# A gdn inverse on 64 by 64 diagonal blocks in quadrants of TensorE's array, and a narrower use of GpSimd for weight low parts

## The chip, the cores and the metric

The kernel is one launch on one core of a Trainium2 chip. The metric is the device time of the launch in microseconds, the median of several runs. Engines are named PE (TensorE, matmuls), PEld (its weight loads), DVE (VectorE), ACT (ScalarE), POOL (GpSimd) and SP (which issues most of the DMAs). SBUF is the on-chip memory of 128 partitions, PSUM the memory that TensorE writes, 8 banks of 128 partitions by 512 floats.

## The reference, cut to what matters

Two models run one after the other on one sequence of 256 tokens with 1024 channels. The first has four layers: gdn (gated delta rule), hgrn, gla, gdn. The second has two layers, here called "four", because four mixers share one projection. Each layer is a projection, a mixer, an output projection, a norm and a gated feed-forward part.

```
def chunk_gated_delta_rule(q, k, v, beta, g):            # the gdn mixer, 8 heads
    ...
    G = jnp.cumsum(g, axis=-1)
    decay = jnp.exp(jnp.where(incl, G[..., :, None] - G[..., None, :], -jnp.inf))
    kb = k * beta[..., None]
    L = jnp.where(strict, jnp.einsum('bhncd,bhnsd->bhncs', kb, k) * decay, 0.0)
    rhs = jnp.concatenate([v * beta[..., None], kb * jnp.exp(G)[..., None]], axis=-1)
    sol = lax.linalg.triangular_solve(L + jnp.eye(CHUNK), rhs, left_side=True, lower=True)
    ...
```

The kernel works with chunks of 128 tokens instead of 64, so it inverts, for each of 8 heads and 2 chunks, the unit lower triangular matrix I + L of 128 by 128: 16 matrices, called problems below.

## The kernel before, in words

**Order of work.** Each engine has its own program, written out by hand, and waits on semaphores that the other engines count up. There is no planner: an engine runs its instructions strictly in the order of the text. `CHAIN` lists the layers: gdn, hgrn, gla, gdn, four, four.

**Projections.** The weights come in units of up to 128 by 2048 floats into a ring of six buffers. Every product is made from three: high part times high part, low times high and high times low, with a weight split into `w_hi` (rounded) and `w_lo` (what is left). The cast to the high part is made by ACT or DVE (`hi_by`, in `unit_plan`), into one of three slots, so it waits until TensorE is done with the unit three before. The low part, ring minus high, is split between two engines: `low_share` eighths of its columns are made by DVE (`split` in the vector program, L1933) and the rest by POOL (`split` in the gpsimd program, L1373). The plan before: from the fourth unit of a layer's projection on (`n >= HI`), DVE casts and makes 2 eighths of the low part, POOL 6 eighths, in every kind of layer. The first three units are cast by ACT, and so are the units of the feed-forward part; there DVE makes the whole low part. TensorE's three products of a unit are at L513 (`products`) and L541 (`token_products`). In hgrn and gla DVE's splits are placed by hand between the steps of its decay work (`due`); in gdn and four they stand ahead of the convolution of the unit that TensorE has finished. ACT's `cast` stands ahead of its work on a unit's output, and does nothing where DVE casts.

**The inverse in a gdn layer.** For each head DVE makes `lt` (the transposed L, 128 by 384 for both chunks and the block across them), from TensorE's products and ACT's Exp. Then the inverse X is built by doubling: at level lv the diagonal blocks of size 2^lv are already inverted, and those of 2^(lv+1) follow. The 16 problems go in four groups g of four. A level has, per group:

- POOL: `masked`, lt times a mask of the level, 128 by 512, into `ct` (L1406); it waits for the cx of the level before;
- PE: `cx` (L881), masked lt times the first halves of X's columns, 64 columns of output per problem;
- ACT: copies cx to `yb`, 128 by 256 (L1413);
- PE: the correction `z` (`gdn_correct`, L952), X transposed times that;
- DVE: subtracts it from X, 128 by 256 (L1887);
- PE: transposes X (`gdn_transpose`, L940), 128 by 128 per problem;
- ACT: copies that to the transposed X in `inv`, 128 by 512 (L1413).

Level 0 has only the mask, DVE's identity minus mask (`first_inverse`) and the transposes. Level 6 has no transposes; it works with the blocks of 64 by 64 (L884, L954), and its correction goes straight into the transposed X. On PE the groups are interleaved: cx of group 0, cx 1, z 0, cx 2, z 1, transposed 0, cx 3, z 2, transposed 1, z 3, transposed 2, transposed 3. `stay_awake` issues matmuls that nothing uses, in places where PE would stand (L585).

Of the kernel before, what the change touches and what calls it, by code (L numbers as in the profile page):

```python
# [29 lines left out]
P = 128  # L30
T = 256
# [181 lines left out]
def build(nc, A, out, book, layers=len(CHAIN)):  # L213

    book.restart()
    with ExitStack() as ctx:
# [42 lines left out]
        ones_d = sb("ones_d", [P, P])  # L259
# [4 lines left out]
        level = sb("level", [P, 7, P])  # L264

# [68 lines left out]
        cx = flat(yb)[:, 0:16 * HALF2].rearrange("p (j n) -> p j n", j=16)  # L334

# [3 lines left out]

        def first_halves(ap, lv):  # L340

            dims = " ".join("abc"[:len(ap.shape) - 2])
            r = ap.rearrange(f"p {dims} (n two c) -> p {dims} n two c", two=2, c=1 << lv)
            return r[:, :, 0, :] if len(ap.shape) == 2 else r[:, :, :, 0, :]
# [141 lines left out]
        def _(pe):  # L486
# [353 lines left out]
            def gdn(layer):  # L840
# [32 lines left out]
                for lv in range(1, 7):  # L873
                    for g in range(4):
                        b = psum.claim(pe, "cx", layer, lv, g)
                        pe.wait_ge(*pool_gdn.at("masked", layer, lv, g))
                        pe.wait_ge(*(act_gdn.at("X", layer, g) if lv == 1 else dve_gdn.at("X", layer, lv - 1, g)))
                        for j in range(4 * g, 4 * g + 4):
                            cols_of = slice((j % 4) * HALF2, (j % 4 + 1) * HALF2)
                            if lv < 6:  # L880
                                m = nc.tensor.matmul(b[:, cols_of].rearrange("p (n c) -> p n c", c=1 << lv),  # L881
                                                     ct[:, j, :], first_halves(inv[:, j, :], lv), start=True, stop=True)
                            else:
                                m = nc.tensor.matmul(b[HALF2:HALF, cols_of], ct[0:HALF2, j, HALF2:HALF], inv[0:HALF2, j, 0:HALF2],  # L884
# [50 lines left out]
            def gdn_transpose(layer, lv, g):  # L935
# [373 lines left out]
        def _(pool):  # L1309
# [21 lines left out]
            fill(ones_d[:, :], 1.0 / D)  # L1331
# [62 lines left out]
            for layer, (kind, _) in enumerate(CHAIN[:layers]):  # L1394
# [6 lines left out]
                for lv in range(7):  # L1401
                    for q in (0, 2, 1, 3) if lv == 0 else range(4):
                        t, h0 = q // 2, 4 * (q % 2)
                        pool.wait_ge(*(dve_gdn.at("lt", layer, h0 + 3) if lv == 0 else
                                       dve_gdn.at("XT", layer, 0, q) if lv == 1 else pe_gdn.at("cx", layer, lv - 1, q)))
                        g.tensor_tensor(ct[:, 4 * q:4 * q + 4, :], lt[:, h0:h0 + 4, t * T:t * T + HALF],  # L1406
                                        level[:, lv:lv + 1, :].to_broadcast([P, 4, HALF]), ALU.mult)\
# [1173 lines left out]
```

## Time and profile before

| | us |
|---|---|
| median of 3 runs (lowest, highest) | 2332.07 (2331.16, 2338.66) |
| the profiled execution | 2331.76 |
| its span, first to last instruction | 2330.1 |
| PE busy | 2213.6 (95%) |
| DVE busy | 1527.5 (66%) |
| ACT busy | 873.9 (38%) |
| POOL busy | 407.5 (17%) |
| mean granted TensorE clock | 0.972 |

The profile is one execution. Busy time is per engine, and engines overlap, so the shares don't add up to the span. A fp32 matmul stands as two records (two passes), and records of matmuls overlap in their durations, so the distance between starts tells what one costs. The granted clock is a share of full speed: 1.00 is 2.4 GHz, 0.50 is 1.2 GHz. The chain of waits goes back from the last instruction to what released it, and so on.

### The profile page before, as it was taken

How to read it: one execution, taken by the hardware profiler on the slowest of the kernel's cores; microseconds unless marked ns; L12 is line 12 of the kernel's file. 1: busy time of each engine (PE TensorE's matmuls, PEld its weight loads, DVE VectorE, ACT ScalarE, POOL GpSimd, SP SyncE). 2: the span in 40 equal slices, each digit the busy share in tenths (PEclk: the TensorE clock that was granted, in tenths of full speed). 3: DMA queues.
4: the chain of work that ended last, by engine and by line, in shares of the span. 5: the costliest groups of instructions: out<-in, count | busy, mean ns of one | idle time of the engine just before them, and what ended most of it. 6: DMA issues, size and time to landing. Idle time of an engine off the chain costs nothing.

```text
span 2330.1 us, 33338 instructions
## 1 busy us (share of the span) xinstructions
PE 2213.6 (95%) x13185; PEld 1915.0 (82%) x13185; DVE 1527.5 (66%) x1923; ACT 873.9 (38%) x1160; POOL 407.5 (17%) x227
## 2 busy tenths in 40 slices
PE   7999999999999999999899999989889999978999
PEld 7988788898788788788798978869568997847998
DVE  7854744797754668645785285466567887367886
ACT  3344444331344322444314444432554333354332
POOL 6632000160000050000262300005120002330000
PEclk9999999999999999999999999999889999979999
DMA  7510565552565443655451056545115554403552
GB/s 213 176 37 25 193 190 189 167 186 64 167 193 182 160 161 97 199 187 174 145 181 55 1 173 194 183 145 165 51 51 173 190 182 134 154 6 114 190 188 91
DMA packets 265597, 333.67 MB, mean 143 GB/s; under 512 B 16492, under 2 KB 228593, under 8 KB 265473
## 3 DMA queue, kind: packets, MB, share of 16 engines
q1 hardware_dynamic: 265473, 331.93, 44.5%
q8 instruction: 89, 1.46, 0.3%
q14 instruction: 35, 0.29, 0.0%
HBM read 330.84 MB, written 1.05 MB: 142 GB/s over the span
## 4 chain that ended last, share of the span: by engine, by line
PE 85%; DVE 9%; ACT 3%; issue 2%; POOL 1%; DVEq 0%; POOLq 0%; ACTq 0%
PE bank L541 42%; PE bank L513 27%; PE bank L952 2%; PE bank L881 2%; PE bank L585 1%; PE bank L1009 1%; DVE w_hi L1931 1%; PE bank L575 1%; PE bank L732 1%; PE bank L940 1%; ACT w_hi L1459 1%; ACT mats L1413 1%; ACT xh L1413 1%; DVE w_lo L1933 1%; PE bank L838 1%
## 5 line engine op out<-in xcount | busy, mean ns | idle before, releaser
L1933 DVE TENSOR_TENSOR w_lo<-ring,w_hi 128x2048 fp32r<-128x2048 f32 (+3 forms) x297 | 561.9, 1893 | 328.5 <-ACT w_hi L1459 325.3
L1459 ACT ACTIVATE w_hi<-ring 128x2048 fp32r<-128x2048 f32 x204 | 385.5, 1890 | 463.2 <-PE bank L541 298.8
L1373 POOL TENSOR_TENSOR w_lo<-ring,w_hi 128x1536 fp32r<-128x1536 f32 (+3 forms) x71 | 277.1, 3903 | 1436.2 <-DVE w_hi L1931 1436.2
L541 PE MATMUL bank<-w_lo,xh 128*128 128x512 f32 x992 | 268.9, 393 | 1.5 <-POOL w_lo L1373 1.4
L541 PE MATMUL bank<-w_hi,xh 128*128 128x512 f32 x928 | 250.9, 392 | 10.6 <-ACT xh L1413 6.8
L513 PE MATMUL bank<-xh,w_lo 128*128 128x256 f32 (+2 forms) x1880 | 246.2, 284 | 5.0 <-POOL w_lo L1373 5.0
L541 PE MATMUL bank<-w_hi,xl 128*128 128x512 f32 x928 | 249.0, 390 | 0.0
L513 PE MATMUL bank<-xh,w_hi 128*128 128x256 f32 (+1 forms) x1816 | 242.7, 287 | 2.3 <-DVE w_hi L1931 2.3
L513 PEld LDWEIGHTS bank<-xh,w_lo 128*128 128x128 f32 (+2 forms) x1880 | 232.2, 188 | 8.0 <-issue 5.7
L513 PEld LDWEIGHTS bank<-xh,w_hi 128*128 128x128 f32 (+1 forms) x1816 | 229.9, 192 | 9.2 <-issue 5.5
L513 PE MATMUL bank<-xl,w_hi 128*128 128x256 f32 (+1 forms) x1816 | 237.2, 283 | 0.0
L513 PEld LDWEIGHTS bank<-xl,w_hi 128*128 128x128 f32 (+1 forms) x1816 | 225.7, 190 | 0.7
L541 PEld LDWEIGHTS bank<-w_lo,xh 128*128 128x128 f32 x992 | 185.8, 189 | 40.6 <-issue 3.0
L541 PEld LDWEIGHTS bank<-w_hi,xh 128*128 128x128 f32 x928 | 173.2, 188 | 50.0 <-issue 11.6
L541 PEld LDWEIGHTS bank<-w_hi,xl 128*128 128x128 f32 x928 | 174.7, 188 | 36.7
L1931 DVE CAST w_hi<-ring 128x2048 fp32r<-128x2048 f32 (+2 forms) x93 | 160.2, 1723 | 43.9 <-PE bank L513 22.9
L541 PE MATMUL bank<-w_hi,hid_hi 128*128 128x512 f32 x528 | 169.0, 401 | 8.1 <-DVE hid_lo L1887 8.1
L541 PE MATMUL bank<-w_hi,hid_lo 128*128 128x512 f32 x528 | 165.0, 394 | 0.0
L541 PE MATMUL bank<-w_lo,hid_hi 128*128 128x512 f32 x528 | 164.4, 393 | 0.0
L1413 ACT ACTIVATE yb<-bank 128x256 f32<-128x256 f32 (+4 forms) x146 | 59.0, 404 | 162.1 <-PE bank L541 124.9
L541 PEld LDWEIGHTS bank<-w_lo,hid_hi 128*128 128x128 f32 x528 | 100.3, 190 | 21.9
L541 PEld LDWEIGHTS bank<-w_hi,hid_lo 128*128 128x128 f32 x528 | 100.0, 189 | 21.9
(310 smaller groups left out, 2605.6 us busy)
## 6 DMA issues: line engine op xcount, KB each, us to landing
ring<-in_ffn_w_in_dram SPq DMA_DIRECT2D x264, 512.0 KB, 4.5
ring<-in_ffn_w_down_dram SPq DMA_DIRECT2D x88, 512.0 KB, 4.3
ring<-in_gdn_w_in_dram SPq DMA_DIRECT2D x64, 512.0 KB, 5.2
ring<-in_ffn_w_out_dram SPq DMA_DIRECT2D x44, 512.0 KB, 4.2
ring<-in_w_in_dram SPq DMA_DIRECT2D x36, 512.0 KB, 4.6
ring<-in_hgrn_w_in_dram SPq DMA_DIRECT2D x32, 512.0 KB, 4.8
ring<-in_gla_w_in_dram SPq DMA_DIRECT2D x24, 512.0 KB, 4.2
ring<-in_gdn_w_out_dram SPq DMA_DIRECT2D x16, 512.0 KB, 4.0
```

Source lines behind the costliest of these rows:

```text
L513: m = nc.tensor.matmul(cols, *((wk, xk) if tokens == ALL else (xk, wk)), start=(first and step == 0 and k == 0 and (j % 2 == 0)), stop=(la ...
L541: m = nc.tensor.matmul(bank[:, 0:width], xin[:, k0 + k, rows_of], w[:, k, c * width:(c + 1) * width], start=(first and step == 0 and k == ...
L575: m = nc.tensor.transpose(b[:, j * P:(j + 1) * P], src[:, t, c * CHUNK + j * P:c * CHUNK + (j + 1) * P], ident[:, :])
L585: m = nc.tensor.matmul(b[:, 0:T], ones[:, :], strict[:, 0:T], start=True, stop=True)
L732: m = nc.tensor.transpose(banks[6][:, j * T + t * HALF:j * T + (t + 1) * HALF], hidt[:, t, j * P:(j + 1) * P], ident[:, :])
L881: m = nc.tensor.matmul(b[:, cols_of].rearrange("p (n c) -> p n c", c=1 << lv), ct[:, j, :], first_halves(inv[:, j, :], lv), start=True, st ...
L952: m = nc.tensor.matmul(b[:, cols], inv[:, 16 + j, :], cx[:, j, :], start=True, stop=True)
L1373: g.tensor_tensor(w_lo[:, unit % RING, part], ring[:, unit % RING, part], high_part(unit)[:, part], ALU.subtract).then_inc(*pool_lo.tick())
L1413: nc.scalar.activation(out_, in_, func, **kw).then_inc(*sig.tick(*key))
L1459: nc.scalar.activation(high_part(u)[:, 0:n], ring[:, u % RING, 0:n], ACT.Copy).then_inc(*act_hi.tick())
L1931: v.tensor_copy(high[:, 0:n], w[:, 0:n]).then_inc(*dve_hi.tick())
L1933: v.tensor_tensor(w_lo[:, u % RING, 0:share], w[:, 0:share], high[:, 0:share], ALU.subtract).then_inc(*dve_lo.tick())
```

## The change

The plan for units: POOL makes low parts only in gdn layers; elsewhere DVE makes all of a unit's low part. In four layers ACT makes all casts. The inverse: up to level 5 only the two 64 by 64 blocks on the diagonal of each problem are kept and worked on, block 0 in partitions 0 to 63 and block 1 in partitions 64 to 127, packed as 64 columns per problem (`xb`, `xtb`, `lb`, `lb_masked`). A matmul of 128 by 128 becomes two of 64 by 64, one in each diagonal quadrant of the array, both into the same PSUM bank. POOL's masks, ACT's copies and DVE's first subtraction are of half the size (128 by 256). ACT copies the diagonal blocks out of lt (8 copies per layer); POOL clears the transposed X; after level 5 ACT spreads the transposed blocks into 128 by 128 tiles, two copies per group. The second block is transposed by a matmul with the identity. Level 6 reads lt itself and doesn't wait for a mask.

```diff
-                unit_plan(KT * w, "dve" if n >= HI else "act", 2 if n >= HI else 8 if layer else 4)
+                unit_plan(KT * w, "act" if n < HI or kind == "four" else "dve", 2 if n >= HI and kind == "gdn" else 8 if layer else 4)
...
+        blocks = (slice(0, HALF2), slice(HALF2, HALF))
+        xb, xtb = (flat(inv[:, 8 * n:8 * n + 8, :]).rearrange("p (j n) -> p j n", j=16) for n in range(2))
+        lb_masked, lb = (flat(ct)[:, 16 * HALF2 * n:16 * HALF2 * (n + 1)].rearrange("p (j n) -> p j n", j=16) for n in range(2))
...
-                        pe.wait_ge(*pool_gdn.at("masked", layer, lv, g))
+                        if lv < 6:
+                            pe.wait_ge(*pool_gdn.at("masked", layer, lv, g))
...
-                                m = nc.tensor.matmul(b[:, cols_of].rearrange("p (n c) -> p n c", c=1 << lv),
-                                                     ct[:, j, :], first_halves(inv[:, j, :], lv), start=True, stop=True)
+                                for r in blocks:
+                                    m = nc.tensor.matmul(b[r, cols_of], lb_masked[r, j, :], xb[r, j, :], start=True, stop=True)
...
-                    m = nc.tensor.transpose(b[:, (j % 4) * P:(j % 4 + 1) * P], inv[:, j + (16 if lv == 0 else 0), :], ident[:, :])
+                    cols_of, src = slice((j % 4) * HALF2, (j % 4 + 1) * HALF2), xtb if lv == 0 else xb
+                    nc.tensor.transpose(b[blocks[0], cols_of], src[blocks[0], j, :], ident[blocks[0], blocks[0]])
+                    m = nc.tensor.matmul(b[blocks[1], cols_of], src[blocks[1], j, :], ident[blocks[1], blocks[1]], start=True, stop=True)
...
-                        m = nc.tensor.matmul(b[:, cols], inv[:, 16 + j, :], cx[:, j, :], start=True, stop=True)
+                        for r in blocks:
+                            m = nc.tensor.matmul(b[r, cols], xtb[r, j, :], cx[r, j, :], start=True, stop=True)
...
-            fill(ones_d[:, :], 1.0 / D)
...
-                for lv in range(7):
+                pool.wait_ge(*act_gdn.at("decay", layer, 0))
+                g.memset(inv[:, 16:32, 0:HALF2], 0.0).then_inc(*pool_gdn.tick("cleared", layer))
+                for lv in range(6):
...
-                        g.tensor_tensor(ct[:, 4 * q:4 * q + 4, :], lt[:, h0:h0 + 4, t * T:t * T + HALF],
-                                        level[:, lv:lv + 1, :].to_broadcast([P, 4, HALF]), ALU.mult)\
+                        g.tensor_tensor(lb_masked[:, 4 * q:4 * q + 4, :], lb[:, 4 * q:4 * q + 4, :],
+                                        level64[:, lv:lv + 1, :].to_broadcast([P, 4, HALF2]), ALU.mult)\
...
+                def diagonal_blocks(g):
+                    t0, h0 = (g // 2) * T, 4 * (g % 2)
+                    act.wait_ge(*dve_gdn.at("lt", layer, h0 + 3))
+                    for r in blocks:
+                        run(s, lb[r, 4 * g:4 * g + 4, :], lt[r, h0:h0 + 4, t0 + r.start:t0 + r.stop], ACT.Copy, "blocks", layer, g)
+
                 for h in range(8):
...
+                    if h in (5, 7):
+                        for g in ((0, 2) if h == 5 else (1, 3)):
+                            diagonal_blocks(g)
...
+                    if lv < 5:
+                        dst, key = (xb, ("X", layer)) if lv == 0 else (xtb, ("XT", layer, lv))
+                        run(s, flat(dst[:, 4 * g:4 * g + 4, :]), b, ACT.Copy, *key, g)
+                    else:
+                        for r in blocks:
+                            run(s, inv[r, 16 + 4 * g:16 + 4 * g + 4, r], b[r, :].rearrange("p (h n) -> p h n", h=4), ACT.Copy, "XT", layer, lv, g)
...
-                            XT = inv[0:HALF2, 16 + 4 * g:16 + 4 * g + 4, HALF2:HALF]
-                            tt(s, XT, XT, b[0:HALF2], ALU.subtract, "XT", layer, lv, g)
+                            ts(s, inv[0:HALF2, 16 + 4 * g:16 + 4 * g + 4, HALF2:HALF], b[0:HALF2].rearrange("p (h n) -> p h n", h=4), -1.0, ALU.mult,
+                               None, None, "XT", layer, lv, g)
```

VectorE's setup also gets four small copies, which pack the identity and the masks to 64 columns.

## Rows read from the trace of the kernel before

**Rows 1.** The page, busy time by engine: us (share of span) xinstructions.
```profile
PE 2213.6 (95%) x13185; PEld 1915.0 (82%) x13185; DVE 1527.5 (66%) x1923; ACT 873.9 (38%) x1160; POOL 407.5 (17%) x227
```

**Rows 2.** Busy time by stretches: from:to, length, engines, PEclk, DMA share, GB/s.
```profile
156.00:165.10 9.10, 8.94 (x83) 8.73 (x81) 1.69 (x4) 3.93 (x8) 7.79 (x7) 1.00 0.00 0
...
1265.00:1271.00 6.00, 4.12 (x25) 3.13 (x25) 4.68 (x5) 1.68 (x3) 5.13 (x4) 1.00 0.01 3
1271.00:1288.00 17.00, 17.00 (x84) 16.88 (x83) 1.69 (x4) 3.75 (x8) 8.17 (x7) 0.50 0.00 0
```

**Rows 3.** Groups by shape, 151.8 to 205.4 us: xcount, busy, mean ns, idle before.
```profile
L952 PE MATMUL bank<-yb,inv 128*128 128x64 f32 x160 | 20.9, 273 | 0.0
...
L940 PE MATMUL bank<-ident,inv 128*128 128x128 f32 x96 | 14.6, 276 | 2.7 <-DVE inv L1887 2.6
...
L1413 ACT ACTIVATE yb<-bank 128x256 f32<-128x256 f32 x20 | 7.7, 384 | 12.0 <-PE bank L881 12.0
```

**Rows 4.** Chain of waits through the levels: start us, us, what.
```profile
156.06 1.74 PE bank L881 x16
...
163.09 0.85 PE bank L952 x8
...
163.97 0.43 DVE inv L1887
...
164.54 0.63 PE bank L940 x4
...
201.58 1.07 PE bank L884 x16
...
1271.65 3.31 PE bank L881 x16
...
1324.70 1.07 PE bank L884 x16
```

**Rows 5.** Stretches of level 6, PE and PEld, L884 alone (two), then L954.
```profile
201.50:202.60 1.10, 1.09 (x16) 1.00 (x16) 1.00 0.00 0
203.00:203.90 0.90, 0.90 (x14) 0.86 (x15) 1.00 0.00 0
...
203.00:203.90 0.90, 0.90 (x15) 0.76 (x12) 1.00 0.00 0
```

**Rows 6.** Chain of waits at the entry of the first inverse.
```profile
150.57 1.28 POOL ct L1406
...
151.87 3.43 DVE inv L1887 x2
```

**Rows 7.** Timeline, ScalarE among the scores: start, us, instruction [idle before].
```profile
145.44 0.52 ACT L1413 ACTIVATE dec<-dec 128x384 f32<-128x384 f32 x1 [1.63 <-DVE dec L1897]
```

**Rows 8.** Timeline of hgrn's projection: DVE, then PE, then POOL.
```profile
448.77 2.28 DVE L1933 TENSOR_TENSOR w_lo<-ring,w_hi 128x2048 fp32r<-128x2048 f32 x1
450.97 1.22 DVE L1931 CAST w_hi<-ring 128x2048 fp32r<-128x2048 f32 x1
...
452.83 4.54 DVE L1931 CAST w_hi<-ring 128x2048 fp32r<-128x2048 f32 x1
...
529.29 2.96 PE L513 MATMUL bank<-xh,w_hi 128*128 128x256 f32 x16 [2.29 <-DVE w_hi L1931]
...
457.45 4.02 POOL L1373 TENSOR_TENSOR w_lo<-ring,w_hi 128x1536 fp32r<-128x1536 f32 x1 [1.16 <-DVE w_hi L1931]
```

**Rows 9.** Timeline of gla's projection: PE, then DVE.
```profile
847.06 2.05 PE L541 MATMUL bank<-w_lo,xh 128*128 128x512 f32 x4 [1.39 <-POOL w_lo L1373]
...
842.91 0.69 DVE L1933 TENSOR_TENSOR w_lo<-ring,w_hi 128x512 fp32r<-128x512 f32 x1
```

**Rows 10.** Chain of waits: a four layer's projection, and a cast on ScalarE.
```profile
1551.10 1.91 ACT w_hi L1459
...
1585.74 54.44 PE bank L513 x456
```

More of the change, by code:

```diff
@@ L334, in build, with bank64 @@
         cx = flat(yb)[:, 0:16 * HALF2].rearrange("p (j n) -> p j n", j=16)
+        blocks = (slice(0, HALF2), slice(HALF2, HALF))
+        xb, xtb = (flat(inv[:, 8 * n:8 * n + 8, :]).rearrange("p (j n) -> p j n", j=16) for n in range(2))
+        lb_masked, lb = (flat(ct)[:, 16 * HALF2 * n:16 * HALF2 * (n + 1)].rearrange("p (j n) -> p j n", j=16) for n in range(2))
+        def bank64(bank):
+            return bank[:, 0:4 * HALF2]
         def prob(n):
             return lt[:, 4 + n % 4, :]
[L340 to L344, printed above, removed]
         def block_ratio(lv, heads):
@@ L1693, in gdn @@
                     run(s, d, d, ACT.Exp, "decay", layer, h)
+                    if h in (5, 7):
+                        for g in ((0, 2) if h == 5 else (1, 3)):
+                            diagonal_blocks(g)
                 def transposed(lv, g):
                     act.wait_ge(*pe_gdn.at("transposed", layer, lv, g))
-                    dst, key = (four_tiles(inv, g), ("X",)) if lv == 0 else (four_tiles(inv, 4 + g), ("XT",))
-                    run(s, dst, psum.bank("transposed", layer, lv, g)[:, :], ACT.Copy, *key, layer, *([lv] if lv else []), g)
+                    b = bank64(psum.bank("transposed", layer, lv, g))
+                    if lv < 5:
[4 more added lines that the diff above has]
+                            run(s, inv[r, 16 + 4 * g:16 + 4 * g + 4, r], b[r, :].rearrange("p (h n) -> p h n", h=4), ACT.Copy, "XT", layer, lv, g)
                     psum.release(s, "transposed", layer, lv, g)
@@ L1949, in setup @@
                 v.tensor_copy(pick[:, :], ident[0:8, 0:8]).then_inc(*s.tick("pick"))
+                for r in blocks:
+                    v.tensor_copy(ident64[r, :], ident[r, r]).then_inc(*s.tick())
+                    v.tensor_copy(level64[r, :, :], level[r, 0:6, r]).then_inc(*s.tick())
                 v.tensor_copy(trig[:, 0, :], pos_i).then_inc(*s.tick())
@@ L2222, in first_inverse @@
                     dve.wait_ge(*pool_gdn.at("masked", layer, 0, g))
-                    tt(s, inv[:, 16 + 4 * g:16 + 4 * g + 4, :], ident[:, :].rearrange("p (a n) -> p a n", a=1).to_broadcast([P, 4, P]),
-                       ct[:, 4 * g:4 * g + 4, :], ALU.subtract, "XT", layer, 0, g)
+                    tt(s, xtb[:, 4 * g:4 * g + 4, :], ident64[:, :].rearrange("p (a n) -> p a n", a=1).to_broadcast([P, 4, HALF2]),
+                       lb_masked[:, 4 * g:4 * g + 4, :], ALU.subtract, "XT", layer, 0, g)
                 for h in range(8):
@@ L2244, in gdn @@
                         dve.wait_ge(*pe_gdn.at("z", layer, lv, g))
-                        b = psum.bank("z", layer, lv, g)[:, 0:4 * HALF2].rearrange("p (h n) -> p h n", h=4)
+                        b = bank64(psum.bank("z", layer, lv, g))
                         if lv < 6:
-                            X = first_halves(inv[:, 4 * g:4 * g + 4, :], lv)
-                            tt(s, X, X, b.rearrange("p h (n c) -> p h n c", c=1 << lv), ALU.subtract, "X", layer, lv, g)
-                        else:
-                            XT = inv[0:HALF2, 16 + 4 * g:16 + 4 * g + 4, HALF2:HALF]
-                            tt(s, XT, XT, b[0:HALF2], ALU.subtract, "XT", layer, lv, g)
+                            X = flat(xb[:, 4 * g:4 * g + 4, :])
+                            tt(s, X, X, b, ALU.subtract, "X", layer, lv, g)
+                        else:
+                            ts(s, inv[0:HALF2, 16 + 4 * g:16 + 4 * g + 4, HALF2:HALF], b[0:HALF2].rearrange("p (h n) -> p h n", h=4), -1.0, ALU.mult,
+                               None, None, "XT", layer, lv, g)
                         psum.release(s, "z", layer, lv, g)
```

9 lines of the change are left out of this document (5 added, 4 removed).

## The prediction

> **What bounds the kernel now.** I read the page first: TensorE is busy 95% of the span [rows 1]. So time is to be had only where TensorE works at something that can be made smaller, or where it stands. The edited code touches two kinds of stretch: the triangular inverse of the two gdn layers, and the projections of the hgrn, gla and four layers. Next the table by stretches [rows 2]: in a level of the first layer's inverse TensorE is busy 8.94 of 9.10 us, so TensorE bounds it. In the second gdn layer the same work runs 17 us at a granted clock of 0.50 (the 1.2 GHz level), right after an entry in which TensorE was busy 4.12 of 6 us. Third the groups of that stretch by shape [rows 3]: what a level is made of. Fourth the chain of waits through the levels [rows 4]: levels 1 to 5 run from 156.06 to 201.58 in the first gdn layer, 45.5 us, and from 1271.65 to 1324.70 in the second, 53.05 us.
>
> **The change part by part.**
>
> *A level of the inverse, before.* An fp32 matmul is two records, a transpose one. The correction has 160 records in 5 levels, cx as many, the transposes 96 in 6 [rows 3]: a level has 32 + 32 + 16 = 80. In the chain 16 records of cx take 1.74 [rows 4], 0.11 us each. 80 x 0.11 = 8.8, plus some 0.3 of waiting: the 9.1 seen.
>
> *A level after.* Each product becomes two of 64 x 64, one in rows and columns 0 to 63, one in 64 to 127: 64 records for cx, 64 for the correction, and 16 transposes + 16 matmuls with the identity = 48, in all 176. What one costs hangs on whether the two quadrants work at the same time. The sixth level already works in quadrants (the two others, crosswise) [rows 5]: alone, 16 records take 1.09 us, 0.068 each; where the two products meet, 14 and 15 records of them lie in the same 0.90 us, 0.062 a pair. I take 0.06 a pair. A group of cx or of the correction then is 8 pairs, 0.48 us (before 0.87); a transposed group is bound by its lower quadrant, 8 records, 0.48 (before 4 x 0.11). Twelve groups give 5.8 us of TensorE a level.
>
> Now the waits, which a shorter TensorE uncovers. From [rows 4]: the level's last correction begins at 163.09, has its 8 records issued 0.11 x 8 later, and VectorE takes it up at 163.97: not over 0.2 us after issue is over, I take 0.2. VectorE runs 0.43, and TensorE starts at 164.54: 0.77 us in all. ScalarE's copy of 128 x 256 takes 0.38 [rows 3], so 0.72. Walking the issue order (cx0, cx1, z0, cx2, z1, T0, cx3, z2, T1, z3, T2, T3): z0 waits for cx0's copy, ready at 0.48 + 0.72 = 1.20 instead of 0.96: 0.24 lost. The other corrections have a group or more between. T3 follows z3 by one group, 0.48, and needs 0.77: 0.29 lost. Level: 5.8 + 0.5 = 6.3 us. ScalarE has 8 copies, 3.0 us, VectorE 4 x 0.43, GpSimd 4 masks at half of 1.28 [rows 6]: all below 6.3, and a mask needs only a cx of the level before. Five levels are 31.5 us: 14.0 saved in the first gdn layer, 21.5 in the second if its clock stays at 1.00. Bounds of a level: 5.5 (nothing waits) and 11.8 (no pair overlaps: 176 x 0.067).
>
> The overlap seen in [rows 5] is of two quadrants that write two banks; here both write one, and no row shows that. The Trainium skill (TensorEngine Tiling, Restrictions and Gotchas) says that different row tiles cannot access the same bank at the same time. By that rule the level would be the upper bound. Its page on PSUM (PSUM bank collisions) lets accesses to different 32-partition quadrants of one bank run side by side, which is this case; by that it is 6.3.
>
> *Entry of the inverse.* Before: behind the last lt GpSimd's mask starts at 150.57 and takes 1.28, VectorE's two subtractions of 128 x 512 follow, 3.43 together, and the last transposes end at 156.06 [rows 6]: 5.5 us. After: ScalarE copies the diagonal blocks, 8 instructions, four of them behind the last lt: 4 x 0.38 = 1.5; the last mask at half size, 0.65; the subtraction at half size, 0.4 to 0.9; then 0.14 and 0.5 of TensorE: 3.2 to 3.7. The other four copies, 1.5 us, lie in ScalarE's gap of 1.63 between two Exps [rows 7]; if they don't fit, one Exp is late by some tenths. 2.0 us saved per layer (bounds 1.0 and 2.8). GpSimd's memset lies in its empty time ahead of the first mask.
>
> *Level 6.* cx reads lt itself and waits for no mask; but ScalarE's last transposed copies become two of 0.38 where one did, and cx0's copy is queued behind them: 0.3 us later. The subtraction becomes a multiplication of the same size: nothing. Cost 0.3 per layer.
>
> *Setup.* One GpSimd memset goes, VectorE gets four small casts, ahead of trigonometry that nothing near waits for: nothing (bounds 0.2 either way).
>
> *Low parts.* In hgrn, gla and four, GpSimd no longer takes three quarters of a unit's low part (13 units in hgrn, 10 in gla, 9 in each four layer). Its instruction of 4.02 us holds up VectorE: the same cast takes 1.22 alone and 4.54 beside it [rows 8]. In hgrn I count six casts and six other VectorE instructions stretched by about 3 us each, 36 us. VectorE now takes 2.28 where it took a quarter, 0.6 to 0.7: 13 x 1.6 = 21 more. It gains 15 us; a unit costs it 3.5 us against 48 x 0.119 = 5.7 of TensorE [rows 10]. What was late: the last unit's cast, TensorE idle 2.29 us and then at the low clock, 16 records in 2.96 instead of 1.9 and some 0.6 more behind them [rows 8]. Both go: 3.9 us (bounds 0 and 4). In gla a larger wait is for ScalarE's gk work and stays; the 1.39 behind GpSimd's low part goes: VectorE is done by 842.91 + 2.28 = 845.2, when the second product, over at 847.06 - 1.39 = 845.7, has not ended [rows 9]: 1.4. In four the projection is an unbroken 54.44 us of TensorE [rows 10]: nothing to win. What it could lose: the casts move to ScalarE, 1.91 us each, behind the Silu of the unit before, which waits for VectorE's convolution. Worked through for unit 7: convolution done 1601.7, cast 1604.4, low part 1606.7, and TensorE comes to it behind one unit of 24 records and four of 48, at 1585.7 + 216 x 0.119 = 1611.4: over 4 us of cover, so nothing. Without that cover each late unit would cost up to 1.9 + 2.3.
>
> **Sum**, against the profiled execution (2331.76 us around a span of 2330.10; the median, 2332.07, is 0.3 above it): 14.0 + 21.5 + 2 x 2.0 - 2 x 0.3 + 3.9 + 1.4 = 44.2. 2331.8 - 44.2 = 2287.6, on the median's footing **2288**.
>
> **Rivals.**
>
> *The clock falls in one inverse* (21%). For: it did in the second layer, whose levels keep TensorE busier than mine will (5.8 of 6.3). Against: the wait ahead of the levels, after which it fell, shrinks, and the first layer kept its clock over the same wait. At the low level a record doubles: 16 of cx take 3.31 where the first layer has 1.74 [rows 4]. A level is then some 11.3 us, and 17 us hold 1.5 levels instead of 2.7: 7.6 lost. 2296.
>
> *The transposes don't pair* (12%). If the upper quadrant's transposes and the lower's matmuls run one after another, a transposed group is 12 x 0.067 = 0.8, a level 7.3: 10 us lost. 2298.
>
> *No pair overlaps, since both quadrants write one bank* (8%): the side of slower. A level 11.8, five are 59 us: 13.5 more in the first layer, 6 more in the second; 4.0 and 5.3 are still won, 0.6 lost: 2332 + 10 = 2342. It decides from 0.10 us a pair on (96 pairs and 0.5 make a level of 10, near the mean of before). Against it speak [rows 5]. The page of the Trainium skill on TensorEngine Tiling, named above, is where its rule stands.
>
> *The clock is at the low level in all of both inverses* (4%), as quadrants fill half the array: 56.5 us each, 11 and 3.5 more, 8.7 won elsewhere: 2338.
>
> *The low parts bring nothing* (3%), as what was late is replaced by another wait on VectorE: 2293.
>
> **How the numbers follow.** The forecast has 52%, its own range 2280 to 2294. 8 times in 10 takes in the first two rivals: 2278 to 2310; the low end is a level of 5.6 and an entry at its better bound. A measurement tells about 0.3% (7 us) from no change. Faster: 52 + 21 + 12 + 3 - 1 for their tails = 0.87; slower 8 + 2 = 0.10 (half of the fourth rival is within the bound); same 0.03.
>
> **What would show it.** 320 records of 64 x 64 each for cx and the correction per gdn layer, two starting together; a level of 6.3 us; level 1 beginning 3.2 to 3.7 after the last lt; granted clock 1.00 in both inverses; in hgrn no GpSimd work, no cast of 4.54 and no idle ahead of the last unit; in gla the wait behind GpSimd gone; four's projection still 54.4. I am wrong if records of a pair lie 0.067 apart, if a level is above 7.5 at clock 1.00 (then a wait that I mis-sized, ScalarE's first), or if TensorE stands in four's projections.

## The result, and the profile after

| | before | after |
|---|---|---|
| median, us (runs) | 2331.61 (4) | 2389.52 (4) |
| lowest, highest | 2330.14, 2338.66 | 2374.56, 2392.83 |
| profiled execution, its span | 2331.76, 2330.1 | 2392.83, 2391.1 |
| PE busy, share | 2213.6, 95% | 2283.3, 95% |
| mean granted clock | 0.972 | 0.946 |

The ratio is 1.0238, 95% interval 1.0205 to 1.027: slower by 58 us. The forecast was 2288.

The page of the changed kernel, its busy row and its clock row, which answer to [rows 1], and behind them the clock row of the kernel before. TensorE has 70 us and 1024 records more (a product is two matmuls now, and half of each transpose is a matmul of two records), GpSimd half of its work. The clock row has an 8 and a 6 (slices 3 and 4, where the first inverse lies) and a 5 and an 8 (the second), where before these four slices had nines.

```profile
PE 2283.3 (95%) x14209; PEld 1953.9 (82%) x14209; DVE 1481.9 (62%) x1909; ACT 903.1 (38%) x1202; POOL 213.2 (9%) x179
...
PEclk9986999999999999999999589999989999979999
...
PEclk9999999999999999999999999999889999979999
```

The groups by shape of the changed kernel from 150 to 236 us, against [rows 3]. L886 is cx, L960 the correction, L946 the transpose of the upper block, L947 the matmul with the identity for the lower. The 320 records of cx and of the correction have about the busy time that the 160 had (21.6 and 21.4 us), mostly at a lower clock. The transposed groups were 14.6 us in all; they are 64.3 now.

```profile
L947 PE MATMUL bank<-ident,inv 64*64 64x64 f32 x192 | 37.9, 288 | 0.0
L946 PE MATMUL bank<-ident,inv 64*64 64x64 f32 x96 | 26.4, 275 | 0.1
L886 PE MATMUL bank<-inv,ct 64*64 64x64 f32 x320 | 21.6, 299 | 0.0
...
L960 PE MATMUL bank<-yb,inv 64*64 64x64 f32 x320 | 21.4, 284 | 0.0
```

Its chain of waits through one transposed group at clock 1.00 and the products behind it, against [rows 4]. Products pair up: 14 and 15 records take 0.41 and 0.47 us, some 0.06 per pair as forecast, with both quadrants writing one bank. But each transpose and its matmul take 0.43 us (starts at 164.84, 165.26, 165.69, 166.12), so a group of four takes 1.7 us where the forecast had 0.48 and the kernel before took 0.44. The last two lines are of a later group at the low clock: a pair takes 0.64 us there and not twice 0.43. The three records of a pair go from 0.06 to 0.11 us each, and what comes on top of them grows only from 0.25 to 0.32 us.

```profile
164.84 0.17 PE bank L946
165.01 0.25 PE bank L947 x2
165.26 0.18 PE bank L946
165.44 0.25 PE bank L947 x2
...
166.12 0.17 PE bank L946
166.29 0.20 PE bank L947
166.55 0.41 PE bank L886 x14
167.01 0.47 PE bank L960 x15
...
172.56 0.24 PE bank L946
172.80 0.40 PE bank L947 x2
```

Stretches of the changed kernel's first inverse (columns as in [rows 2]): TensorE counts as busy in every microsecond, and its clock goes between the two levels and then stays near the lower one. A level starts every 13.2 us, the last two every 17.1. From 160.58 to 234.39 the five levels take 73.8 us (before 45.5). In the second inverse the first level takes 13.2 and the other four 17.1, from 1303.26 to 1384.70, 81.4 us (before 53.05).

```profile
154.00:164.00 10.00, 10.00 (x110) 7.89 (x111) 1.24 (x2) 2.30 (x6) 4.21 (x6) 0.69 0.01 2
164.00:170.00 6.00, 6.00 (x91) 4.70 (x88) 1.15 (x3) 1.53 (x4) 1.45 (x2) 0.94 0.00 0
...
197.00:239.00 42.00, 42.00 (x432) 33.57 (x433) 4.42 (x11) 9.79 (x26) 2.90 (x4) 0.52 0.00 1
```

Where the time went, from the starts in the two chains: first gdn mixer 34.7 us longer, second (with its projection) 34.9, setup 1.1 longer, hgrn's projection 4.7 shorter (84.7 to 80.0), gla's 2.9 shorter, four's 54.44 as before. That makes 63 us, and the spans differ by 61: the other 2.2 went around the first four layer, outside its projection (its norm starts 63.1 us later than before, its output projection 60.9).

### The profile page after: what moved, and what is told of

Read it like the earlier page. It is cut to its first block, busy times and chain, and to the rows that moved or that the text cites. A ratio compares the mean times of both kernels' runs of the same rounds, so it can differ in the third digit from the quotient of the medians.

```text
span 2391.1 us, 35321 instructions
## 1 busy us (share of the span) xinstructions
PE 2283.3 (95%) x14209; PEld 1953.9 (82%) x14209; DVE 1481.9 (62%) x1909; ACT 903.1 (38%) x1202; POOL 213.2 (9%) x179
## 4 chain that ended last, share of the span: by engine, by line
PE 88%; DVE 6%; ACT 3%; issue 2%; POOL 1%; DVEq 0%; POOLq 0%; ACTq 0%
PE bank L544 42%; PE bank L516 27%; PE bank L947 3%; PE bank L946 2%; PE bank L588 2%; PE bank L960 1%; PE bank L886 1%; PE bank L1017 1%; PE bank L578 1%; PE bank L735 1%; PE bank L827 1%; ACT w_hi L1467 1%; ACT stat L1421 1%; ACT mats L1421 1%; ACT xh L1421 1%
## 5 line engine op out<-in xcount | busy, mean ns | idle before, releaser
L1956 DVE TENSOR_TENSOR w_lo<-ring,w_hi 128x2048 fp32r<-128x2048 f32 (+3 forms) x297 | 625.6, 2108 | 364.3 <-ACT w_hi L1467 361.7
L1467 ACT ACTIVATE w_hi<-ring 128x2048 fp32r<-128x2048 f32 (+1 forms) x222 | 417.8, 1882 | 486.9 <-PE bank L544 304.0
L544 PE MATMUL bank<-w_hi,xh 128*128 128x512 f32 x928 | 250.5, 392 | 10.6 <-ACT xh L1421 6.8
L1380 POOL TENSOR_TENSOR w_lo<-ring,w_hi 128x1536 fp32r<-128x1536 f32 (+1 forms) x30 | 117.4, 3916 | 1017.7 <-DVE w_hi L1954 1017.7
L544 PEld LDWEIGHTS bank<-w_lo,hid_hi 128*128 128x128 f32 x528 | 100.3, 190 | 21.8
L544 PEld LDWEIGHTS bank<-w_hi,hid_hi 128*128 128x128 f32 x528 | 95.4, 190 | 26.6 <-DVE hid_lo L1910 10.7
```

The source lines that it names most:

```text
L544: m = nc.tensor.matmul(bank[:, 0:width], xin[:, k0 + k, rows_of], w[:, k, c * width:(c + 1) * width], start=(first and step == 0 and k == ...
L1380: g.tensor_tensor(w_lo[:, unit % RING, part], ring[:, unit % RING, part], high_part(unit)[:, part], ALU.subtract).then_inc(*pool_lo.tick())
L1467: nc.scalar.activation(high_part(u)[:, 0:n], ring[:, u % RING, 0:n], ACT.Copy).then_inc(*act_hi.tick())
L1956: v.tensor_tensor(w_lo[:, u % RING, 0:share], w[:, 0:share], high[:, 0:share], ALU.subtract).then_inc(*dve_lo.tick())
```

## The experiments

### The two halves of the change, each alone

The low parts alone (the kernel before with the new plan of units):

```diff
-                unit_plan(KT * w, "dve" if n >= HI else "act", 2 if n >= HI else 8 if layer else 4)
+                unit_plan(KT * w, "act" if n < HI or kind == "four" else "dve", 2 if n >= HI and kind == "gdn" else 8 if layer else 4)
```

> The kernel before with the second part of the change alone: GpSimd takes a share of the low parts in gdn projections only, the inverse as before. From the stretches of the two traces (hgrn projection 84.7 to 80.0 us, gla 70.1 to 67.2, four's the same) this is worth 7.6 us: about 2324, ratio 0.9967. The forecast had 5.3 us: 2326. Rival: part of the 4.7 and 2.9 us in the changed kernel comes from other things moved by the inverse (a later start with filled buffers), and the edit alone gives under 3 us: 2329 or more.

Measured: 2322.56 against 2331.12, ratio 0.9956 (0.9933 to 0.9979): 8.6 us won, by the interval 5 to 16. Its own trace has the 4.7 us in hgrn and 3.1 in gla. It also shows something of the clock: the inverse in it is that of the kernel before, but here the 17 us at clock 0.50 lie in the first inverse (156 to 173 us) and the second has 1.00, the reverse of [rows 2]. So where that stretch falls differs from one execution to another.

```profile
156.00:173.00 17.00, 17.00 (x83) 16.88 (x83) 1.69 (x4) 4.36 (x9) 7.60 (x7) 0.50 0.00 1
```

The inverse alone is the changed kernel with that line taken back.

> The changed kernel with the low parts shared as before: the inverse on quadrants alone. If the parts are additive it is 7.6 us slower than the changed kernel's 2389.5, at about 2397, 65 us over the kernel before. If the low parts interact with the inverse (through GpSimd, whose casts in the stages around it share its time with DVE), the two single edits' differences don't sum to the 58 us measured for both, by more than 5 us.

Measured: 2398.42 (2384.86 to 2417.32), ratio 1.031 (1.0259 to 1.0362), 67.3 us lost. The halves add up: 67.3 - 8.6 = 58.7 against 57.9, closer than the spread of these four runs can show. So the whole loss is the inverse's. The low parts brought at least what was forecast; that they brought more rests on the traces, since the interval of the times takes in the 5.3.

### No transposes

```diff
-                    nc.tensor.transpose(b[blocks[0], cols_of], src[blocks[0], j, :], ident[blocks[0], blocks[0]])
-                    m = nc.tensor.matmul(b[blocks[1], cols_of], src[blocks[1], j, :], ident[blocks[1], blocks[1]], start=True, stop=True)
+                    for r in blocks:
+                        m = nc.tensor.matmul(b[r, cols_of], src[r, j, :], ident[r, r], start=True, stop=True)
```

> The changed kernel, but the upper quadrant's block is also transposed by a matmul with the identity, so that the inverse holds no transpose at all on TensorE after the entry. Theory A (alternating between transposes and matmuls is what the forecast mis-sized): a transposed group takes what a products' group takes, 0.48 us at full clock, a level 6.3 us, and the kernel comes to the forecast of 2288, or 2290 to 2296 with the setup's 1.1 us and one stretch at the low clock. Theory B (a transposed block of float32 at 64 rows is slow in any form): the group stays above 1 us, the kernel above 2330. Theory C (the clock falls because quadrant work counts for less, transposes or not): a level of 16 records per group at clock 0.50 takes about 11.5 us, the two inverses about 115 to 125 us together, the kernel 2338, as the forecast's rival of a low clock had it.

Measured: 2294.14 (2290.65 to 2299.95), ratio 0.984 (0.9809 to 0.9872). Making the 192 transposes of the two inverses matmuls of two passes wins 95 us over the changed kernel. Theory A holds. (In these 95 us are both the price of alternating and the low clock; the split stands further down.) The chain of this kernel (L947 is now the whole transposed group, L960 the correction) shows the group at 0.47 us and what is left to wait for, VectorE's last subtraction (0.43) and 0.14 behind it:

```profile
171.40 0.47 PE bank L947 x16
171.87 0.47 PE bank L886 x16
...
174.16 0.43 DVE inv L1910
174.59 0.14 issue
174.73 0.68 PE bank L947 x16
175.41 0.93 PE bank L886 x32
```

The stretch that holds the second layer's levels in it, at the clock that the forecast's first rival and its fourth had doubted:

```profile
1248.00:1283.00 35.00, 32.70 (x992) 31.00 (x992) 8.82 (x21) 17.61 (x47) 13.75 (x20) 1.00 0.01 4
```

### The same eight instructions, fewer changes

First all four transposes of a group, then its four matmuls:

```diff
                 for j in range(4 * g, 4 * g + 4):
...
                     nc.tensor.transpose(b[blocks[0], cols_of], src[blocks[0], j, :], ident[blocks[0], blocks[0]])
+                for j in range(4 * g, 4 * g + 4):
+                    cols_of = slice((j % 4) * HALF2, (j % 4 + 1) * HALF2)
                     m = nc.tensor.matmul(b[blocks[1], cols_of], src[blocks[1], j, :], ident[blocks[1], blocks[1]], start=True, stop=True)
```

> The changed kernel, but a group of four transposed blocks issues its four transposes of the upper quadrant first and then its four matmuls with the identity on the lower one: the same eight instructions, and one alternation per group instead of four. Theory A (the price is in alternating: in the changed kernel's trace each step from a transpose to a matmul or back costs some 0.11 to 0.18 us more than the instructions themselves, 0.43 us per pair at granted clock 1.00): the group falls from 1.7 us to about 0.9 to 1.1 at full clock, a level from 13.2 us to about 8.5 to 9, the two inverses together from 147 us to about 90, the kernel to 2320 to 2335. Theory B (a transpose of a 64 by 64 block takes about 0.4 us of the array by itself, whatever stands beside it): the group stays at 1.7 us or grows, since nothing runs beside the transposes, and the kernel stays at 2380 to 2395. Theory C (it is the low granted clock that lengthens everything in the inverse, and the clock falls because only a quadrant is at work at a time): groups at 1.00 don't change, the clock stays at 0.5 to 0.9 in the inverse, and the time stays within 15 us of the changed kernel's.

Measured: 2306.53, ratio 0.9895 (0.9865 to 0.9926). The instructions are the same as in the changed kernel; their order alone is worth 83 us, the clock's share among them. In its chain (L947 the transposes, L950 the matmuls, some of whose records run on beside cx) four transposes take 0.34 us, so B falls; by its table of stretches, in the second fence, the clock of the first inverse is 1.00 (it is 0.95 over 1240 to 1275 us, in the second), so C falls too:

```profile
174.17 0.47 PE bank L963 x16
174.63 0.34 PE bank L947 x4
174.97 0.43 PE bank L950 x5
175.58 0.29 PE bank L886 x10
```

```profile
164.10:195.00 30.90, 30.68 (x704) 27.73 (x700) 6.74 (x16) 13.14 (x35) 8.56 (x12) 1.00 0.01 3
```

Where all eight records of L950 stand alone they take 0.60, so a group takes 0.34 + 0.60 = 0.94 us. Theory A's working of it: four transposes at 0.06, four matmuls alone at 0.12, two changes at 0.12. I had expected 2320 to 2335, having set a level at 8.5 to 9; it is 7.8.

### Changes inside one quadrant

```diff
-                    nc.tensor.transpose(b[blocks[0], cols_of], src[blocks[0], j, :], ident[blocks[0], blocks[0]])
+                    if j % 2:
+                        nc.tensor.matmul(b[blocks[0], cols_of], src[blocks[0], j, :], ident[blocks[0], blocks[0]], start=True, stop=True)
+                    else:
+                        nc.tensor.transpose(b[blocks[0], cols_of], src[blocks[0], j, :], ident[blocks[0], blocks[0]])
+                for j in range(4 * g, 4 * g + 4):
...
                     m = nc.tensor.matmul(b[blocks[1], cols_of], src[blocks[1], j, :], ident[blocks[1], blocks[1]], start=True, stop=True)
```

> The changed kernel, but a group alternates inside the upper quadrant (transpose, matmul with the identity, transpose, matmul), and the lower quadrant's four matmuls follow. Theory A (a change of mode costs about 0.12 us whichever quadrants are used): upper part 2 x 0.06 + 2 x 0.12 + four changes x 0.12 = 0.84, lower part 0.47 beside nothing: 1.2 to 1.3 us a group, level about 9.5, kernel about 2320 to 2335, the clock perhaps below 1.00. Theory A2 (only a change that also moves to the other quadrant costs): 0.36 + 0.47 = 0.83 us or less, kernel 2300 to 2306.

Measured: 2322.85 (2320.49 to 2329.2), ratio 0.996 (0.9944 to 0.9977). Theory A. A level at full clock starts every 8.9 us (157.25, 166.15); less eight product groups of 0.47 that leaves 1.28 per transposed group. The pace is the changed kernel's though both instructions are in the upper quadrant (L949 the transpose, L947 the matmul there, L952 the lower quadrant):

```profile
159.90 0.17 PE bank L949
160.07 0.26 PE bank L947 x2
...
160.50 0.20 PE bank L947
160.75 0.18 PE bank L952 x4
```

From the fourth level on its granted clock is below 1.00 as well, with TensorE busy all the time; in the second inverse it is 0.83 from 1260 to 1280 us:

```profile
185.00:195.00 10.00, 10.00 (x191) 8.87 (x190) 1.68 (x4) 2.94 (x9) 2.27 (x4) 0.84 0.01 2
```

### The same alternation on the full array, in the kernel before

```diff
-                    m = nc.tensor.transpose(b[:, (j % 4) * P:(j % 4 + 1) * P], inv[:, j + (16 if lv == 0 else 0), :], ident[:, :])
+                    block, src = b[:, (j % 4) * P:(j % 4 + 1) * P], inv[:, j + (16 if lv == 0 else 0), :]
+                    if j % 2:
+                        m = nc.tensor.matmul(block, src, ident[:, :], start=True, stop=True)
+                    else:
+                        nc.tensor.transpose(block, src, ident[:, :])
```

> The kernel before, with every second 128 by 128 transpose of the inverse made by a matmul with the identity instead, so that a group alternates between transposes and matmuls four times over. A transpose takes 0.11 us there and a 128-column float32 matmul of this kind 0.23, so without any price of alternating a group goes from 0.44 to 0.68 us. Theory A (any change between transposing and multiplying costs about 0.12 us): a group takes 0.68 plus three or four changes, about 1.1 us, a level 2.6 us more, the kernel about 2331 + 2 x 6 x 2.6 = 2362, less if it hides. Theory A2 (the price belongs to changing the quadrant together with the mode, and a full-array change is free, as nothing in the kernel before shows one): a group 0.68, a level about 1 us more, the kernel 2331 + 12 = 2343. The clock: if it was alternation that let the granted clock fall in the changed kernel, it falls here too under A and not under A2.

Measured: 2332.64 against 2331.5, ratio 1.0 (0.9982 to 1.0018). The first inverse is as A2 had it, somewhat better: level 6 begins at 204.9 us where it began at 201.5, 0.7 a level, since part of the longer group fills the wait at a level's end [rows 4]. The second inverse gives it back in the profiled run: the 17 us at clock 0.50 of [rows 2] aren't there, the same stretch has 142 records instead of 84, and level 6 begins 1.5 us earlier than before. One trace can't say that the edit did this, since that stretch moves between executions of the unchanged inverse too; but the ten runs have a mean clock of 0.971 to 0.977, the kernel before 0.967 to 0.974.

```profile
1271.00:1288.00 17.00, 15.87 (x142) 15.44 (x141) 4.29 (x7) 7.17 (x15) 13.59 (x11) 1.00 0.01 1
```

The price per change is in the chain: a transpose takes 0.11 us (L944), a matmul 0.22 (L942), one behind the other, and nothing between.

```profile
160.44 0.12 PE bank L944
160.56 0.22 PE bank L942 x2
160.78 0.11 PE bank L944
...
161.11 0.84 PE bank L881 x8
```

So a change between transposing and multiplying is free on the full array and costs some 0.12 us among matmuls on quadrants. The price isn't the transpose mode's as such.

### Quadrants and full array in turn, without a transpose

The edit is against the kernel without transposes.

```diff
                     for r in blocks:
-                        m = nc.tensor.matmul(b[r, cols_of], src[r, j, :], ident[r, r], start=True, stop=True)
+                        nc.tensor.matmul(b[r, cols_of], src[r, j, :], ident[r, r], start=True, stop=True)
+                    m = nc.tensor.matmul(b[:, 4 * HALF2:5 * HALF2], flat(src[:, 4 * g:4 * g + 2, :]), ident[:, 0:HALF2], start=True, stop=True)
```

> The kernel with both blocks transposed by matmuls, and after each head's two quadrant matmuls one matmul on the full array more (128 by 128 weights, 64 columns, float32, result not read): a group alternates four times between the array in quadrants and the whole array, with no transpose in it. It tells apart what a change in the changed kernel consisted of. Theory A (leaving the quadrants and coming back is what drains the array, and a float32 transpose of 64 by 64 makes it do that): four pairs 0.47 us, four full matmuls 4 x 0.22 = 0.88 or half of that, and eight changes of about 0.12, in all about 2.3 us a group and a low clock beside: kernel 2294 + 48 x 1.8 = 2380 or more. Theory B (only the transpose mode among quadrant matmuls costs, a change between quadrants and the full array is free): 0.47 + 0.9 = 1.35 us, kernel 2294 + 48 x 0.88 = 2336.

Measured: 2409.96, ratio 1.0321 (1.0276 to 1.0367). Theory A again. Its timeline at clock 1.00 (start, duration, instruction; L947 a pair of quadrant matmuls, L948 the one on the full array):

```profile
190.15 0.33 PE L947 MATMUL bank<-ident,inv 64*64 64x64 f32 x4
190.41 0.43 PE L948 MATMUL bank<-ident,inv 128*128 128x64 f32 x2
190.77 0.33 PE L947 MATMUL bank<-ident,inv 64*64 64x64 f32 x4
```

The quadrant pair holds the engine 0.26 us where it takes 0.12 among its like, the full matmul 0.37 where two of its records take 0.22: 0.14 and 0.15 us for each change of the array's shape, with no transpose about. That is close to the changed kernel's 0.17 - 0.06 and 0.25 - 0.12 per transpose. So a float32 transpose of 64 by 64 behaves as if it took the array out of its quadrants; that it does so is an inference from the equal prices. The Trainium skill has a rule that fits it (TensorEngine Tiling, Restrictions and Gotchas, among the feature incompatibilities): column tiling is mutually exclusive with transpose mode for FP32 input. It doesn't say what becomes of such a transpose; here it runs and costs two changes. I had weighed that section's rule on banks, which the traces don't bear out here, and passed over this one.

### Why the clock fell

This edit too is against the kernel without transposes.

```diff
+                for k in range(10):
+                    m = nc.tensor.matmul(b[blocks[0], 4 * HALF2 + 4 * k:4 * HALF2 + 4 * k + 4], src[blocks[0], j, :], ident[blocks[0], 0:4],
+                                         start=True, stop=True)
                 m.then_inc(*pe_gdn.tick("transposed", layer, lv, g))
```

> The kernel with both blocks transposed by matmuls, and after each transposed group ten further matmuls of four columns (float32, upper quadrant, results not read), which keep PE's queue busy with next to no columns: about as long as alternation held it in the changed kernel (1.2 us a group), without a single transpose. It tells apart why the granted clock fell in the changed kernel's inverse. Theory A (it fell because the array multiplies little while instructions follow one another, whatever the cause): ten matmuls take about 0.6 to 1.2 us, a level about 9 to 11 us at full clock, and the granted clock falls to 0.5 to 0.9 in the levels as it did there: kernel 2345 to 2390. Theory B (the clock fell because of the changes between transposing and multiplying as such): the clock stays at 1.00 and the kernel takes 2294 + 48 groups x 0.6 to 1.2 us, 2323 to 2350.

Measured: 2367.36 against 2330.08, ratio 1.0147 (1.011 to 1.0185), above B's 2350. The ten matmuls take 1.06 us at full clock. A level with them takes 10.5 us at full clock where the kernel without them has 6.6, since they also fill its waits; with the two entries that is some 47 of the 73 us between the two kernels, and some 26 are the clock's, an estimate by difference. With no transpose in it, it has low stretches as the changed kernel had, from the entry on, but also three tens of us at 1.00, the middle line one of them:

```profile
154.00:164.00 10.00, 10.00 (x166) 10.00 (x167) 0.78 (x1) 2.30 (x6) 3.96 (x6) 0.64 0.01 2
...
184.00:194.00 10.00, 9.93 (x265) 9.82 (x265) 1.68 (x4) 2.88 (x8) 2.86 (x4) 1.00 0.01 3
...
204.00:214.00 10.00, 10.00 (x198) 10.00 (x199) 0.84 (x2) 2.85 (x8) 0.00 (x0) 0.66 0.01 3
```

And the kernel before with every second transpose a matmul kept 1.00 from 155 to 200 us. So the fall needs no changes of shape and no transposes. Nor do changes of shape bring it everywhere. The kernel with a full-array matmul between the quadrant pairs, which has eight changes in every transposed group, is at 0.70 and 0.79 from 154 to 174 us and at 1.00 from 174 to 214:

```profile
184.00:194.00 10.00, 10.00 (x134) 8.18 (x132) 0.84 (x2) 1.53 (x4) 0.73 (x1) 1.00 0.01 2
```

What the runs show is that the clock fell in stretches in which TensorE was "busy" all along with four-column matmuls or with changes of shape in between, and in some such stretches did not. Theory A gave the time and the size of the fall, but not the levels at 1.00 in both kernels. Why the clock came back up in the middle of these inverses and not in the changed kernel's, these runs leave open.

### A better version

Two edits on the kernel without transposes. First VectorE's four setup copies go from the head of the angles' chain to layer 0's gdn stage:

```diff
+                if layer == 0:
+                    for r in blocks:
+                        v.tensor_copy(ident64[r, :], ident[r, r]).then_inc(*s.tick())
+                        v.tensor_copy(level64[r, :, :], level[r, 0:6, r]).then_inc(*s.tick())
```

> The kernel in which both blocks are transposed by matmuls (the one expected at the forecast's 2288, measured 2294.1), with DVE's four setup copies (ident64, level64) moved from the head of the angles' chain into layer 0's gdn stage, behind the copy of cols. Theory: the copies are stretched by GpSimd (2.25 and 2.57 us for the last two), push the angles and the first residual low cast back, and leave PE idle 0.80 us at 44.6: the move gives back 1.1 to 1.4 us, 2292.8. Rival: PE's wait at that place is set by other work (ACT's rows, GpSimd's slot), and the time stays at 2294.

The cause, in VectorE's timeline of the changed kernel: the first two copies, of the same shapes, take 0.17 and 0.34 us; the last two are stretched to 2.25 and 2.57 us while GpSimd makes two low parts (L1380, 4.98 us from 19.02 on), and TensorE then stands 0.80 us for a cast behind the angles:

```profile
19.47 2.25 DVE L1974 COPY ident<-ident 64x64 f32<-64x64 f32 x1
21.64 2.57 DVE L1975 COPY level<-level 64x384 f32<-64x384 f32 x1
...
44.64 2.15 PE L516 MATMUL bank<-xh,w_hi 128*128 128x256 f32 x16 [0.80 <-DVE w_hi L1954]
```

With the copies moved, the same matmuls start 1.40 us earlier:

```profile
43.24 2.15 PE L516 MATMUL bank<-xh,w_hi 128*128 128x256 f32 x16 [0.36 <-DVE w_hi L1954]
```

In whole runs 2293.2 against 2294.1 (in another set of runs): the trace shows the gain, the times alone couldn't. Second, a level's last transposed group goes behind the next level's first product:

```diff
                         m.then_inc(*pe_gdn.tick("cx", layer, lv, g))
+                        if g == 0 and lv > 1:
+                            gdn_transpose(layer, lv - 1, 3)
...
                         gdn_transpose(layer, lv, 2)
-                        gdn_transpose(layer, lv, 3)
```

> The kernel with matmul transposes and the setup copies moved, and in addition a level's last transposed group is issued behind the next level's first product (ACT's copy likewise). In the matmul version PE waits 0.5 to 0.6 us at each level's end for DVE's subtraction of the last group (0.43) to land before it can transpose it; a product of 0.47 us fits there. Theory: 10 level ends x 0.4 to 0.5 us: 4 to 5 us under the version without it, about 2288. Rival: the correction that follows then waits for ACT's copy of the later transpose, and nothing is won.

Measured: 2287.78 (2284.27 to 2291.99), ratio 0.9817 (0.9793 to 0.9841): 5.4 us under the version before it (2288.61 to 2295.9, measured on the same chip), as expected, 43.7 under the kernel before and 101.7 under the changed one. Its chain (L948 the transposed group, L961 the correction) has no wait at the level's end; a level is twelve groups of 0.47, 5.6 us, and with the waits that are left the ten levels take 57.8:

```profile
159.40 0.47 PE bank L948 x16
159.86 0.47 PE bank L886 x16
160.33 0.47 PE bank L948 x16
...
165.46 0.47 PE bank L886 x16
```

## Why the prediction was wrong, step by step

*The failed step* is this one of "A level after": "a transposed group is bound by its lower quadrant, 8 records, 0.48". It is 1.7 us at full clock. I priced every record of the changed inverse by the neighbours of its own shape in level 6 [rows 5], where only matmuls stand, and took it for granted that a transpose pairs with them as a matmul does. The rival "the transposes don't pair" doubted the overlap, but its 0.8 us still had no price for the alternation. With 0, 2, 4 and 8 changes per group a level takes 5.6 to 7.0, 7.8, 8.9 and, by its parts at full clock, 10.6 us (4 x (0.47 + 0.47 + 1.7)). The sign "a level above 7.5 at clock 1.00" came, but its reading there, a mis-sized wait with ScalarE's first, was wrong: by its records TensorE was never idle in the levels.

*Its size.* 95.4 us lie between the changed kernel and the one without transposes. 48 groups x (1.7 - 0.47) are 59. The ten levels without transposes take 66.4 us where their groups are 56, so some 10 us of waits stand in that kernel which the longer groups cover: 49 are left. The remaining 46 are the clock, an estimate by difference. The levels' starts say nearly the same: ten of 10.6 would be 106 us, and they take 73.8 + 81.4 = 155.2, 49 more. So about half of the 95 us is the mis-sized group and half the clock that came with it. I had a rival for a fall in one inverse and one for both, both with levels of 6.3 us of quadrant matmuls and nothing else. Such levels kept the clock at 1.00 in both inverses of the three kernels without transposes; where it fell in the other kernels on quadrants, changes of shape or four-column matmuls stood between them.

*The products* were right: 0.47 per group of 8 pairs against 0.48, though both quadrants write one bank. By the Trainium skill's rule on banks (TensorEngine Tiling, Restrictions and Gotchas), named in the prediction, different row tiles cannot access one bank at the same time; no kernel here bears that out. With the failed step taken out, a level is 6.3 to 7.0 against 6.3, and from the first transpose of v to u0 the first mixer takes 63.8 us against 77.1, the second 63.0 against 84.8: 13.3 and 21.8 won, where the forecast's 14.0 + 2.0 - 0.3 and 21.5 + 2.0 - 0.3 were 15.7 and 23.2.

*The entry:* the order of the parts came as worked out, but each was longer. In the version without transposes ScalarE's last four copies take 1.7 us (1.5 forecast), GpSimd's mask 0.91 (0.65) and VectorE's subtraction 0.94 (0.4 to 0.9), and level 1 begins 4.5 us after the last lt, where 3.2 to 3.7 were forecast and 5.5 was the time before. That is 1.0 won. From the first transpose of v, cx begins 26.2 us later instead of 27.8: 1.6 won, 2.0 forecast, so another 0.5 came ahead of the last lt, which the forecast didn't name. In the changed kernel the sixteen transposes of the entry and their matmuls took 7.8 us and ate it.

*The low parts:* 5.3 forecast, 7.6 by the traces, 8.6 (5 to 16) by the times. hgrn gave 4.7 (3.9 forecast, whose upper bound was 4), gla 2.9 (1.4 forecast): there the wait behind GpSimd went as worked out, and the other waits of that stretch (3.5 and 0.8 us) stand in both traces. The other 1.5 us is the clock. Behind the 3.5 us wait it was low in both kernels, but it stayed low for longer in the kernel before, where the second wait follows (847.06 in [rows 9]): from the first of the twelve products behind the waits to the next unit TensorE took 15.7 us there, 14.3 without the wait, and 12.7 in the changed kernel. The forecast priced a low clock behind the wait in hgrn and left it out in gla. The first line is of the kernel before, the second of the changed one, both some 3 to 8 us behind the start of the first product (843.02 and 874.20):

```profile
846.00:850.00 4.00, 2.94 (x7) 2.39 (x8) 2.63 (x2) 1.15 (x2) 0.92 (x1) 0.50 0.00 0
...
878.00:882.00 4.00, 4.00 (x18) 3.29 (x18) 3.08 (x2) 0.70 (x2) 0.00 (x0) 0.99 0.00 0
```

Four stayed at 54.44, as forecast.

*Setup:* forecast at nothing, with 0.2 either way; it was 1.1 to 1.4. I had seen VectorE stretched beside GpSimd in hgrn [rows 8] and used it there, and did not ask what GpSimd does while the setup copies run: it makes low parts.

*The sum* of 44.2 us was nearly reached in the end (43.7, 2287.8), by a kernel without the alternation, which the forecast had left out without noticing: the reordering, which the forecast didn't have, and what the low parts gave beyond the forecast make up for what level and entry fell short. That it meets 2288 so closely is luck.

## What to carry to other kernels

Where an instruction is priced by its neighbours in a trace, look whether a neighbour of another shape or mode stands between them: on quadrants of the array a float32 transpose or a full-array matmul cost 0.11 to 0.15 us at each change at full clock, and order alone moved this kernel by 83 us. If blocks are worked on in quadrants, transpose them there by a matmul with the identity, though it takes twice the passes, or gather the transposes. When a section of the Trainium skill is read for one of its rules, weigh each line of it against every instruction that the change adds.

## What the runs showed of the hardware that I had not expected

- Quadrant and full-array matmuls in turn: 0.14 us extra into the full array, 0.15 back. At the low clock it is 0.20 each way (from 158.30 on the starts are 0.41 and 0.61 us apart, where the records alone would take 0.21 and 0.41): the records double, the change doesn't. Transposes and matmuls of 128 by 128 in turn: nothing (0.11 and 0.22 us).
- Matmuls of four columns in one quadrant follow each other at 0.053 us a record (20 in 1.06), nearly the 0.059 of 64 columns: little is gained by fewer columns. The same holds on the full array, where a record of 64 columns (cx, 16 in 1.74) and one of 128 (a transpose) both take 0.11 us. Each of these records has a weight load of its own (the page counts as many loads as records). With 64 columns a record takes 0.11 us with weights of 128 by 128 and 0.059 with 64 by 64, so up to 128 columns its time goes with the size of the weights.
- A granted clock of 0.52 to 0.94 over 85 us in which TensorE was at no time idle by its records. Busy in the page is no sign that the clock is safe.
- Two diagonal quadrants writing one bank overlap fully: 16 records in 0.47 us, in every group of cx and of the correction.
